# Spilled expert gates by first key, second key and token: 256 B runs in the write, 2 KB runs in the read

## The reference

```python
expert_idx = ...          # first key * 128 + second key, (T, 8, 16)
gates = jax.nn.softmax(best_s, axis=-1)
u = jnp.take(expert_u, ib, axis=0)
act = jax.nn.gelu(jnp.einsum('td,thkd->thk', xb, u))
w = (gb * act)
v = jnp.take(expert_v, ib, axis=0)
return jnp.einsum('thk,thkd->td', w, v)
```

## Time and profile before

| | |
|---|---|
| Time, median of 3 runs | 3117.32 us (3115.15 to 3118.13) |
| Span of the profiled execution | 3116.1 us; no other time is given for it |
| PE busy | 3062.9 us, 98% |
| POOL, DVE, ACT busy | 75%, 62%, 23% |
| DMA packets | 245,544, of them 145,601 under 512 B |
| Stage with the gate lots | about 1040 to 1706 us |
| Second layer of the experts | about 1752 to 2445 us |

### The profile page before, as it was taken

The page is one execution under the profiler, slowest core; times in us unless marked ns, Lnnn a source line. Parts: engine busy times, 40 slices in busy tenths (PEclk is TensorE's granted clock), DMA queues, the critical chain, the costliest instruction groups (busy, mean ns, idle before and its releaser), DMA issues.

```text
span 3116.1 us, 40637 instructions
## 1 busy us (share of the span) xinstructions
PE 3062.9 (98%) x13738; PEld 2470.8 (79%) x13738; DVE 1942.4 (62%) x2787; ACT 715.2 (23%) x1255; POOL 2334.2 (75%) x1127
## 2 busy tenths in 40 slices
PE   7999999999999999999999999999999999899998
PEld 6788877788878888888888888888888775678886
DVE  6488656221253788988876467676767567876621
ACT  3244223220022122121222111111111266332201
POOL 6834654677776888898999888888888762478876
PEclk9999999999999999999999999999999999999999
DMA  4211221223322455444555766666666421122222
GB/s 146 89 54 48 98 75 58 74 94 122 108 95 86 141 186 186 171 157 176 186 182 211 224 188 188 188 188 189 188 188 188 132 75 34 43 91 97 94 94 74
DMA packets 245544, 405.63 MB, mean 130 GB/s; under 512 B 145601, under 2 KB 145729, under 8 KB 244161
## 3 DMA queue, kind: packets, MB, share of 16 engines
q1 hardware_dynamic: 224560, 331.68, 33.9%
q10 hardware_dynamic: 20880, 72.62, 6.0%
HBM read 335.04 MB, written 69.21 MB: 130 GB/s over the span
## 4 chain that ended last, share of the span: by engine, by line
PE 93%; DVE 4%; POOL 1%; issue 1%; ACT 1%; DMA 0%; POOLq 0%; SPq 0%; ACTq 0%; DVEq 0%
PE bank L598 20%; PE bank L600 20%; PE bank L599 20%; PE banks L598 6%; PE banks L600 6%; PE banks L599 6%; PE banks L898 2%; PE banks L749 2%; PE banks L711 1%; PE banks L713 1%; PE banks L712 1%; PE banks L814 1%; PE bank L775 1%; PE banks L805 1%; POOL w_lo L506 1%
## 5 line engine op out<-in xcount | busy, mean ns | idle before, releaser
L504 POOL TENSOR_TENSOR w_hi<-w_raw,ones 128x1024 fp32r<-128x1024 f32 x492 | 955.6, 1942 | 713.9 <-PE bank L600 478.5
L506 POOL TENSOR_TENSOR w_lo<-w_raw,w_hi 128x1024 fp32r<-128x1024 f32 x492 | 1232.0, 2504 | 38.6
L598 PE MATMUL bank<-h_hi,w_hi 128*128 128x512 f32 x2000 | 792.3, 396 | 8.1 <-DVE h_lo L1889 7.0
L600 PE MATMUL bank<-h_hi,w_lo 128*128 128x512 f32 x2000 | 780.1, 390 | 0.0
L599 PE MATMUL bank<-h_lo,w_hi 128*128 128x512 f32 x2000 | 778.9, 389 | 0.0
L598 PEld LDWEIGHTS bank<-h_hi,w_hi 128*128 128x128 f32 x2000 | 376.0, 188 | 91.4 <-DVE h_lo L1889 13.9
L600 PEld LDWEIGHTS bank<-h_hi,w_lo 128*128 128x128 f32 x2000 | 375.4, 188 | 80.3
L599 PEld LDWEIGHTS bank<-h_lo,w_hi 128*128 128x128 f32 x2000 | 375.9, 188 | 74.8 <-issue 2.2
L2376 DVE TENSOR_TENSOR ew_lo<-expert_w,ew_hi 128x512 fp32r<-128x512 f32 x128 | 249.3, 1987 | 184.6 <-ACT ew_hi L1593 180.8
L2372 DVE TENSOR_TENSOR expert_w<-acts_in,gates_in 128x512 f32<-128x512 f32 x128 | 243.3, 1937 | 66.4 <-DMA gates_in<-gates 51.6
L2305 DVE TENSOR_TENSOR hot<-bank,tab 128x512 fp32r<-128x512 f32 x256 | 164.5, 684 | 85.0 <-PE banks L898 84.3
(11 more groups left out here) (444 smaller groups left out, 4571.9 us busy)
## 6 DMA issues: line engine op xcount, KB each, us to landing
w_raw<-weights SPq DMA_DIRECT2D x494, 512.0 KB, 3.5
acts<-act_out_stage ACTq DMA_DIRECT2D x128, 256.0 KB, 2.8
gates<-gate_stage ACTq DMA_DIRECT2D x8, 4096.0 KB, 12.9
acts_in<-acts SPq DMA_DIRECT2D x128, 256.0 KB, 4.2
gates_in<-gates SPq DMA_DIRECT2D x128, 256.0 KB, 4.6
resid<-x SPq DMA_DIRECT2D x4, 512.0 KB, 8.3
resid<-x ACTq DMA_DIRECT2D x4, 512.0 KB, 8.2
out<-final SPq DMA_DIRECT2D x3, 512.0 KB, 2.6
```

Of the source, the lines that this page charges most:

```text
L504: nc.gpsimd.tensor_tensor(w_hi[:, pair, :], w_raw[:, slot, :], one_col.to_broadcast((P, 1024)), ALU.mult).then_inc(hi_split, 1)
L506: nc.gpsimd.tensor_tensor(w_lo[:, pair, :], w_raw[:, slot, :], f32(w_hi[:, pair, :]), ALU.subtract).then_inc(split_done, 1)
L598: mm(out_, hi, rhs_hi, start=first, stop=False)
L600: return mm(out_, lo, rhs_hi, start=False, stop=last)
```

## The change

The DRAM tensor is ordered by first key, second key and token. A lot's write now cuts each partition's 32 KB into 128 runs of 256 B, one for each first key, which lie 256 KB apart in DRAM (128 second keys by 512 tokens by 4 B). A key's read finds all 512 tokens of a partition in one run of 2 KB. Bytes, number of transfers, their places in the program, semaphores and buffers are the same. The read's access pattern takes fewer register instructions on SP. Lines after L450 have numbers lower by one.

```diff
-    gates = nc.dram_tensor("gates", (T // STAGED_TOKENS, NKEYS, NKEYS, STAGED_TOKENS), F32, kind="Internal").ap()
+    gates = nc.dram_tensor("gates", (NKEYS, NKEYS, T), F32, kind="Internal").ap()
...
-            sp.dma_start(g_in[:, slot, :].rearrange("p (b t) -> p b t", t=STAGED_TOKENS),
-                         gates[:, :, bass.ds(e, 1), :].rearrange("b k a t -> k b (a t)")).then_inc(gate_in[slot], 16)
+            sp.dma_start(g_in[:, slot, :], gates[bass.ds(e, 1), :, :].rearrange("a k t -> (a k) t")).then_inc(gate_in[slot], 16)
...
-                    act.dma_start(gates[lot:lot + 1, :, :, :].rearrange("b k a t -> k (b a t)"),
-                                  stage[:].rearrange("p a t -> p (a t)")).then_inc(gates_out, 16)
+                    act.dma_start(gates[:, :, lot * STAGED_TOKENS:(lot + 1) * STAGED_TOKENS].rearrange("a k t -> k a t"),
+                                  stage[:]).then_inc(gates_out, 16)
```

## The result

The changed kernel takes 3184.23 us (median of 4 runs, 3182.61 to 3184.70) against 3117.73 us (4 runs), a ratio of 1.0216 with a 95% interval of 1.0202 to 1.0231: 66.5 us slower. The span of the profiled execution went from 3116.1 to 3182.7 us.

The account below looks back on a forecast made before the run. PE, busy 98% of the span, was taken as the bound. Seven stalls of 9.0 us and one of 8.6 made 71.6 us; 3116.1 + 71.6 = 3187.7, plus 1.2 for the median, gave 3189 us, range 3145 to 3350.

Parts of the forecast that it names:

- PE has no gain on the read: Second layer's gate read: costs and gains PE nothing; landing up to 0.5 us earlier only shortens DVE's 19.0 us wait.
- The landing, L = 24.9 us: Time from a lot's write issue to its landing: 18.4 us runs, 4.7 weight loads, 1.8 fixed, against 13.3 before.
- The stall, L - 15.9: PE's wait behind a lot landing L after issue: 9.0 us for seven lots, 8.6 for the last (L - 16.3).
- ACT is held at its next issue: Rival, chance 0.12: ACT's issue behind a lot stays until about L - 2; PE stalls L - 12.7, 95 us, 3212.
- Dearer short writes: Rival, chance 0.33: 256 B writes cost two passes, 36 ns each; lots land after 45.1 us, 233 us slower, 3350.
- The turn to the second layer: SP's loads behind the last lot wait until 24.9 us after its issue, no later for PE, itself 8.6 us late.

Follow-up runs that it names:

- the read alone: Second layer reads 2 KB runs while lots are still written in 32 KB runs, against the kernel before: 3117.77 us, ratio 1.0004.
- the two versions issued by SP: SP instead of ACT issues the lots' writes: the changed kernel so altered takes 3150.76 us, the version with 8,192 runs of 512 B 3119.16 us.
- ACT issuing later: Changed kernel with ACT issuing each lot behind the first tile of its last step instead of ahead of it: 3167.40 us, ratio 1.0160.

## Why the prediction was right, and where not

- **Sign and size.** 3189 us were forecast and 3184 measured, 71.6 us against 66.5. The range and the sign held. That the sum was near is luck, as two errors cancelled: a landing that was too late and a mechanism that was too cheap.
- **PE has no gain on the read.** Right: the read alone is 1.0004. DVE's wait for the gates in the second layer went from 19.0 us to 8.1, and PE didn't notice.
- **The landing, L = 24.9 us.** Wrong, 19.1. Two terms of it were too large. The price of a run was put at 18 ns from the packets' busy time; that is right as busy time (1.274 x 64/4,530 gives 18.0 ns, and the earlier trace rows gave the same for reads), but packets overlap, and the pace is 14.1 ns. The earlier trace rows held a warning, 16.7 ns apart, which I used only for the lower end. And the weight loads were counted with 3 x 1.6 = 4.7 us; 2.8 are left for them (19.1 less 1.8 less 14.5). By the packets in each us, only two whole ones fall within the first lot: they bring its 1,132 packets a us down to 94 (1150.87 to 1151.87 us) and 101 (1155.87 to 1156.87), and take some 1.25 us each, an estimate from these counts.
- **The stall, L - 15.9.** As a threshold for the first batch it is right, as the two versions issued by SP show (3.0 us for an L of 19.0, 0.1 for 16.0). It left out the second batch of the pair, which waits for the second sum and allows 0.5 us less. In the changed kernel it wasn't what bound. With L = 19.1 it would have given 3.2 us a lot and 3143 us.
- **ACT is held at its next issue.** I gave this rival 0.12 on the evidence of one issue of 0.93 us. It is what happened. Its formula, L - 12.7, gives 6.4 us for L = 19.1, and the gap was 6.4 us (6.59 between starts less 0.23). As a rule it is too coarse: ACT comes free not 2 us before the landing but when few runs are left, which for 512 B is 2.4 to 4.4 us before. The runs 320 B apart test both formulas at the forecast's own L: with lots that land after 24.9 us the gap was 10.1 us, at the tile and not at the batches, against 9.0 by the forecast and 12.2 by this rival.
- **Not in the forecast: the clock.** 1.5 to 2.6 us in each of the eight lots, 17 us together or a quarter of the loss. That a stall would slow what follows it stood in no term of mine. My expectation for the lots issued by SP had it as 0 to 2.1 us, and it came in six of seven.
- **Dearer short writes.** Refuted. The Trainium skill, DMA: Bandwidth & Descriptors, section Specifications, has a read-modify-write below 512 B; by the pace of 256, 512 and 1,024 B here, which lies on one straight line, no second pass is paid for. Whether one takes place is not shown.
- **The turn to the second layer.** Right: SP's loads came no later for PE; the last lot cost its own stall and nothing more.

## What to carry to other kernels

A layout that shortens runs on one side and lengthens them on the other is judged by who waits on each side, not by the number of packets: both had 131,072 short ones. Behind a transfer of thousands of runs, look at the next issue on the same queue; the engine that makes it stands still, and the cheap remedies are longer runs (1 KB sufficed), another issuing queue, or doing first what others wait for. For the time of a many-run transfer count the pace at which packets start, not their busy time, and where PE will idle for some us, add the slow clock behind it.

## What the runs showed of the hardware

- An issue behind a transfer of thousands of runs is held until few of them are left. In the first lot of the versions with 256 B, 512 B and 1 KB these are 1,100 to 1,200 runs, 69 to 76 for each engine. ACT's queue behind the end of the hold, all packets by size: for 256 B (1158.11 to 1160.5 us)

```profile
DMA packets 1160, 0.50 MB, mean 209 GB/s; under 512 B 1106, under 2 KB 1106, under 8 KB 1160
```

  for 512 B (1152.67 to 1157.3 us; those between 512 B and 2 KB are the lot's)

```profile
DMA packets 1648, 1.66 MB, mean 357 GB/s; under 512 B 62, under 2 KB 1270, under 8 KB 1648
```

  and for 1 KB (1149.92 to 1155.5 us)

```profile
DMA packets 1501, 2.21 MB, mean 397 GB/s; under 512 B 47, under 2 KB 1175, under 8 KB 1501
```

  It is no fixed number: over the eight lots of the changed kernel 21 to 105 for each engine were left, over all versions 17 to 109. That the queue's depth sets it is an inference.
- Only the queue that issued the lot is held. SP's weight loads took 0.33 us to issue while ACT stood still. They landed later, though: those issued 4.7 and 10.3 us behind the first lot took 6.9 and 6.5 us, against 3.5 and 3.7 for the two ahead of it.
- PE's granted clock fell to 0.50 behind every gap of 3.9 us and more (31 in four kernels), behind seven of the eight of 2.6 to 3.3 us (SP issuing, and the last lot with ACT issuing later), and behind one of the seven of 1.4 to 2.2 us (512 B). Behind the gaps of 5.9 to 7.2 us of the changed kernel it cost 1.7 to 2.6 us each.
- Runs of 256 B laid 320 B apart, three in four of which don't start at a multiple of 256 B, take 18.9 ns on an engine on average, instead of 14.1.
- A write of 256 B, 512 B and 1 KB runs starts one every 14.1, 23.5 and 42.4 ns on an engine.
